# Reordering the first loads of a one-core decoder trunk

## The reference

```
xn = rmsnorm(h, mixer_norm[0])
h  = h + retention(xn, ret_w_in, ret_w_out)      # 4 heads, q and k rotated by cos/sin tables
h  = h + hier_moe(rmsnorm(h, ffn_norm[0]), ...)  # 32 experts, 2 per token
k_sh, v_sh = shared_kv(h, kv_norm, w_kv, k_norm)
h  = h + dilated_attention(rmsnorm(h, mixer_norm[1]), k_sh, v_sh, ...)
h  = h + hier_moe(rmsnorm(h, ffn_norm[1]), ...)
```

## Time and profile before

| | |
|---|---|
| median of 3 runs | 1517.93 us (1515.38 to 1518.26) |
| profiled execution | 1517.55 us, span 1515.7 us |
| TensorE busy | 1186.6 us, 78% of the span |
| VectorE, ScalarE | 434.6 us (29%), 340.7 us (22%) |
| DMA | 489.02 MB, mean 323 GB/s |

### The profile page before, as it was taken

The page is one execution under the profiler, slowest core; times in us unless marked ns, Lnnn a source line. Parts: engine busy times, 40 slices in busy tenths (PEclk is TensorE's granted clock), DMA queues, the critical chain, the costliest instruction groups (busy, mean ns, idle before and its releaser), DMA issues.

```text
span 1515.7 us, 16138 instructions
## 1 busy us (share of the span) xinstructions
PE 1186.6 (78%) x6928; PEld 712.2 (47%) x6928; DVE 434.6 (29%) x834; ACT 340.7 (22%) x560; POOL 64.8 (4%) x119
## 2 busy tenths in 40 slices
PE   4999996858667667576999899996857677577575
PEld 4986785413323133132788767776413133133131
DVE  4754535100100101003766534635100101001001
ACT  3334422101001001012655444642101001001010
POOL 2000000000000000000300051030000000000000
PEclk8999997988878898797999989996988789688888
DMA  8552476999999999998545554457999999999996
GB/s 307 180 195 103 193 277 234 420 421 421 421 421 422 421 421 421 422 421 349 146 167 184 203 110 123 172 168 312 373 421 421 421 421 421 422 421 422 421 421 264
DMA packets 90778, 489.02 MB, mean 323 GB/s; under 512 B 6385, under 2 KB 6449, under 8 KB 41041
## 3 DMA queue, kind: packets, MB, share of 16 engines
q1 hardware_dynamic: 86736, 480.55, 78.7%
q0 software_dynamic: 3968, 7.42, 2.8%
HBM read 486.77 MB, written 1.17 MB: 322 GB/s over the span
## 4 chain that ended last, share of the span: by engine, by line
PE 58%; DMA 34%; DVE 4%; issue 1%; SPq 1%; ACT 1%; POOL 0%; ACTq 0%; DVEq 0%
DMA ring<-in_exp_down 20%; DMA ring_more<-in_exp_down 13%; PE bank L1004 8%; PE triple L1043 7%; PE triple L344 7%; PE triple L345 7%; PE triple L346 7%; PE bank L1079 4%; PE triple L1060 4%; PE bank L1060 2%; PE bank L344 2%; PE bank L346 2%; PE bank L345 2%; DMA ring<-in_ret_w_in 1%; PE bank L1426 1%
## 5 line engine op out<-in xcount | busy, mean ns | idle before, releaser
L1043 PE MATMUL triple<-ring,work 128*32 128x512 f32 x1344 | 251.4, 725 | 84.9 <-DMA ring<-in_exp_up 53.5
L1043 PE MATMUL triple<-ring_more,work 128*32 128x512 f32 x704 | 161.0, 720 | 38.8 <-DMA ring<-in_exp_up 25.6
L1043 PEld LDWEIGHTS triple<-ring,work 128*32 128x32 f32 x1344 | 63.9, 129 | 218.4 <-issue 218.4
L1153 DVE TENSOR_TENSOR work<-work,triple 128x512 f32<-128x512 f32 x16 | 11.0, 688 | 529.3 <-PE triple L1043 529.3
L1060 PE MATMUL triple<-ring,work 128*32 128x512 f32 x344 | 93.8, 910 | 78.5 <-DMA ring<-in_exp_down 41.6
L1004 PE MATMUL bank<-work,hn 128*128 128x128 f32 x512 | 125.8, 407 | 16.5 <-DVE h L1162 12.2
L1004 PEld LDWEIGHTS bank<-work,hn 128*128 128x128 f32 x512 | 123.2, 335 | 27.9 <-issue 23.4
L1162 DVE TENSOR_TENSOR h<-h,bank 128x512 f32<-128x512 f32 x64 | 44.0, 687 | 279.7 <-PE bank L1079 279.7
L326 DVE TENSOR_TENSOR lo_b<-ring,hi_b 128x2048 fp32r<-128x2048 f32 x40 | 90.0, 2288 | 21.3 <-ACT hi_b L319 21.3
L1043 PEld LDWEIGHTS triple<-ring_more,work 128*32 128x32 f32 x704 | 39.2, 128 | 102.9 <-issue 102.9
L1060 PE MATMUL triple<-ring_more,work 128*32 128x512 f32 x168 | 60.2, 922 | 33.4 <-DMA ring<-in_exp_down 29.5
(11 more groups left out here) (280 smaller groups left out, 1791.3 us busy)
## 6 DMA issues: line engine op xcount, KB each, us to landing
ring<-in_exp_down SPq DMA_DIRECT2D x43, 2048.0 KB, 32.6
ring<-in_exp_gate SPq DMA_DIRECT2D x42, 2048.0 KB, 32.9
ring<-in_exp_up SPq DMA_DIRECT2D x42, 2048.0 KB, 33.0
ring_more<-in_exp_gate SPq DMA_DIRECT2D x22, 2048.0 KB, 32.9
ring_more<-in_exp_up SPq DMA_DIRECT2D x22, 2048.0 KB, 33.5
ring_more<-in_exp_down SPq DMA_DIRECT2D x21, 2048.0 KB, 32.5
ring<-in_ret_w_in SPq DMA_DIRECT2D x12, 2048.0 KB, 9.3
ring<-in_w_kv SPq DMA_DIRECT2D x12, 2048.0 KB, 8.8
```

What stands on the lines that cost most here:

```text
L1043: last = nc.tensor.matmul(bank[2 + kind][rows, :], m_x[:, k, rows], w[e][:, kk * FF:(kk + 1) * FF], start=(k == 0), stop=(k == KD - 1))
```

## The change

SyncE now issues x, the first weight tile in two halves with a semaphore each, the rotation tables, and then the other tiles. ScalarE's queue issues the identity and the mixer gains on a semaphore of their own. The rest of the small loads are issued by GpSimd after a wait for the first tile. The splitting of tile 0 is laced with the norm and the transposes: low half 0 before them on VectorE, high half 0 before `x_hi` on ScalarE, the other halves behind. TensorE starts on k = 0, 1 when the first batch of `x_lo` is there. ScalarE takes a root right at the start, from a memset tile. In the router, two pairs of semaphores become one pair.

```diff
+        s_ident = sem("identity_and_first_gain_loaded")
+        s_first = sem("first_half_tile_loaded")
+        s_rot = sem("rotation_tables_loaded")
+        s_one = sem("table_operand_set")
...
         def split_act(act, n, parts=(0, 1)):
+            if n == 0:
+                act.wait_ge(s_ring[0] if 1 in parts else s_first, 16)
             if 0 in parts:
-                act.wait_ge(s_ring[slots_in_order[n]], 16 * loads_through(n))
+                if n > 0:
+                    act.wait_ge(s_ring[slots_in_order[n]], 16 * loads_through(n))
...
-            nc.scalar.activation(root_of_no_use[0:1, i:i + 1], h[0:1, 0, 0:1], ACT.Sqrt, scale=0.0)
+            if i > 0:
+                nc.scalar.activation(root_of_no_use[0:1, i:i + 1], h[0:1, 0, 0:1], ACT.Sqrt, scale=0.0)
...
         def retention_pe(pe):
-            xT_ready(pe, 0)
...
                             if hh == 0 and half == 0 and k % 4 == 0:
                                 half_ready(pe, n, k // 4)
+                            if i == 0 and half == 0 and k % 2 == 0:
+                                pe.wait_ge(s_xT_dve, k // 2 + 1)
...
         def retention_act(act):
-            for n in range(-2, 4):
+            for n in range(-1, 4):
...
         def retention_dve(dve, chain):
-            for n in range(-2, 0):
-                split_next(split_dve, dve, n, DENSE_A - 1)
-            dve.wait_ge(r_tab, 16 * 3)
+            split_next(split_dve, dve, -1, DENSE_A - 1)
+            dve.wait_ge(s_rot, 16)
...
             def decayed(hd):
                 dve.wait_ge(r_s_done, hd + 1)
+                dve.wait_ge(r_tab, 16)
...
-            act.wait_ge(s["top_in"], 1)
-            nc.scalar.activation(m_t[:, 1, 0:2], m_t[:, 1, 0:2], ACT.Exp).then_inc(s["top_out"], 1)
+            act.wait_ge(s["exp_in"], 2)
+            nc.scalar.activation(m_t[:, 1, 0:2], m_t[:, 1, 0:2], ACT.Exp).then_inc(s["exp_out"], 1)
...
         @block.sync
             sp.dma_start(h[:, :, :], x[0].rearrange("(t p) d -> p t d", p=P)).then_inc(s_x, 16)
-            sp.dma_start(kept[:, :], constants[:, 0:C_KEPT]).then_inc(s_small, 16)
-            sp.dma_start(gains[:, 0:4:2, :], mixer_norm ...).then_inc(s_small, 16)
-            sp.dma_start(gains[:, 1:4:2, :], ffn_norm ...).then_inc(s_small, 16)
-            sp.dma_start(gains[:, 4, :], kv_norm ...).then_inc(s_small, 16)
-            for i in range(N_WIN):
+            first = ring[:, 0, :].rearrange("p (k c) -> p k c", k=KD)
+            sp.dma_start(first[:, 0:KD // 2, :], win[:, 0:KD // 2, 0:COLS]).then_inc(s_first, 16)
+            sp.dma_start(first[:, KD // 2:KD, :], win[:, KD // 2:KD, 0:COLS]).then_inc(s_ring[0], 16)
+            sp.dma_start(work[:, 16384:16384 + 2 * S], constants[:, C_COS:C_COS + 2 * S]).then_inc(s_rot, 16)
+            for i in range(1, N_WIN):
                 load_tile(sp, FIRST_WIN + i, win[:, :, i * COLS:(i + 1) * COLS], KD)
...
         @block.gpsimd
-            pool.dma_start(r_cos, constants[:, C_COS:C_COS + S]).then_inc(r_tab, 16)
-            pool.dma_start(r_sin, constants[:, C_SIN:C_SIN + S]).then_inc(r_tab, 16)
+            pool.wait_ge(s_ring[0], 16)
+            pool.dma_start(kept[:, P:C_KEPT], constants[:, P:C_KEPT]).then_inc(s_small, 16)
+            pool.dma_start(gains[:, 1:4:2, :], ffn_norm ...).then_inc(s_small, 16)
+            pool.dma_start(gains[:, 4, :], kv_norm ...).then_inc(s_small, 16)
...
         @block.scalar
+            act.dma_start(kept[:, 0:P], constants[:, 0:P]).then_inc(s_ident, 16)
+            act.dma_start(gains[:, 0:4:2, :], mixer_norm ...).then_inc(s_ident, 16)
+            act.wait_ge(s_one, 1)
+            nc.scalar.activation(root_of_no_use[0:1, 0:1], root_of_no_use[0:1, 1:2], ACT.Sqrt)
             norm_act(act, 0)
-            act.wait_ge(s_small, 64)
+            split_act(act, 0, (0,))
+            act.wait_ge(s_ident, 32)
             transpose_act(act, 0, (x_hi, x_lo), 0)
+            split_act(act, 0, (1,))
             retention_act(act)
+            act.wait_ge(s_small, 16 * 3)
...
         @block.vector
+            nc.vector.memset(root_of_no_use[:, :], 1.0).then_inc(s_one, 1)
             norm_dve(dve, chain, 0)
-            dve.wait_ge(s_small, 64)
+            split_dve(dve, 0, (0,))
+            dve.wait_ge(s_ident, 32)
             transpose_dve(dve, 0, (x_hi, x_lo), 0)
+            split_dve(dve, 0, (1,))
+            dve.wait_ge(s_small, 16 * 3)
             retention_dve(dve, chain)
...
         @block.tensor
-            pe.wait_ge(s_small, 64)
+            pe.wait_ge(s_ident, 32)
             transpose_pe(pe, 0)
```

More of the change, by code:

```diff
@@ L767, in build @@
         for layer in range(2):
-            names = ("logits", "exp_in", "exp_out", "top_in", "top_out", "chosen", "ranked", "slots_ready",
+            names = ("logits", "exp_in", "exp_out", "chosen", "ranked", "slots_ready",
                      "route_w", "step")
@@ L921, in route_dve @@
             V.tensor_tensor(A, hot1, hot2, ALU.add).then_inc(s["chosen"], 1)
-            V.tensor_tensor(m_t[:, 1, 0:2], top2, top1, ALU.subtract).then_inc(s["top_in"], 1)
+            V.tensor_tensor(m_t[:, 1, 0:2], top2, top1, ALU.subtract).then_inc(s["exp_in"], 1)
             psum, r = tmp(TT), tmp(TT)
@@ L926, in route_dve @@
             chain(V.tensor_reduce(psum, m_t[:, 0, 0:8].rearrange("p (t g) -> p t g", t=TT), AX, ALU.add))
-            dve.wait_ge(s["top_out"], 1)
+            dve.wait_ge(s["exp_out"], 2)
             chain(V.tensor_scalar(r, m_t[:, 1, 0:2], 1.0, None, ALU.add))
@@ L1835, in _ @@
             sp.dma_start(h[:, :, :], x[0].rearrange("(t p) d -> p t d", p=P)).then_inc(s_x, 16)
-            sp.dma_start(kept[:, :], constants[:, 0:C_KEPT]).then_inc(s_small, 16)
-            sp.dma_start(gains[:, 0:4:2, :], mixer_norm.rearrange("l (p k) -> p l k", k=KD)).then_inc(s_small, 16)
-            sp.dma_start(gains[:, 1:4:2, :], ffn_norm.rearrange("l (p k) -> p l k", k=KD)).then_inc(s_small, 16)
-            sp.dma_start(gains[:, 4, :], kv_norm.rearrange("(p k) -> p k", k=KD)).then_inc(s_small, 16)
-            for i in range(N_WIN):
+            first = ring[:, 0, :].rearrange("p (k c) -> p k c", k=KD)
[3 more added lines that the diff above has]
+            for i in range(1, N_WIN):
                 load_tile(sp, FIRST_WIN + i, win[:, :, i * COLS:(i + 1) * COLS], KD)
@@ L1879, in route_loads @@
                                ).then_inc(s, 16)
-            pool.dma_start(r_cos, constants[:, C_COS:C_COS + S]).then_inc(r_tab, 16)
-            pool.dma_start(r_sin, constants[:, C_SIN:C_SIN + S]).then_inc(r_tab, 16)
+            pool.wait_ge(s_ring[0], 16)
+            pool.dma_start(kept[:, P:C_KEPT], constants[:, P:C_KEPT]).then_inc(s_small, 16)
+            pool.dma_start(gains[:, 1:4:2, :], ffn_norm.rearrange("l (p k) -> p l k", k=KD)).then_inc(s_small, 16)
+            pool.dma_start(gains[:, 4, :], kv_norm.rearrange("(p k) -> p k", k=KD)).then_inc(s_small, 16)
             pool.dma_start(work[:, 16896:16896 + RET_H * DECAY_W],
@@ L1918, in _ @@
         def _(act):
+            act.dma_start(kept[:, 0:P], constants[:, 0:P]).then_inc(s_ident, 16)
+            act.dma_start(gains[:, 0:4:2, :], mixer_norm.rearrange("l (p k) -> p l k", k=KD)).then_inc(s_ident, 16)
+            act.wait_ge(s_one, 1)
+            nc.scalar.activation(root_of_no_use[0:1, 0:1], root_of_no_use[0:1, 1:2], ACT.Sqrt)
             norm_act(act, 0)
-            act.wait_ge(s_small, 64)
+            split_act(act, 0, (0,))
+            act.wait_ge(s_ident, 32)
             transpose_act(act, 0, (x_hi, x_lo), 0)
+            split_act(act, 0, (1,))
             retention_act(act)
+            act.wait_ge(s_small, 16 * 3)
             norm_act(act, 1)
```

## The result

| | before | changed |
|---|---|---|
| median of 6 runs | 1516.32 us (1514.56 to 1518.26) | 1508.59 us (1506.24 to 1509.72) |
| ratio, 95% interval | | 0.9947 (0.9934 to 0.9960) |
| profiled execution, span | 1517.55, 1515.7 | 1509.11, 1507.3 |

The change makes the kernel 7.7 us faster by the medians, 8.4 by the two spans.

The account below looks back on a forecast made before the run. The start was taken as bound by the order of bytes, with time won before 38 us passing through whole. Earlier resumption 5.76, twelve early matmuls 1.43 and clock 0.5 sum to 7.7: 1510.2 us, range 1506.5 to 1514.0.

Parts of the forecast that it names:

- x: Load of x at the start: lands at 5.3 us instead of 5.73, with about 0.16 MB less ahead of it.
- First half: First half of the first weight tile: lands 2.7 us after x, at 8.0 us; upper bound 10.7.
- Norm: First norm on ScalarE: early root moves the table load, so root and scaling come 1.1 us earlier; hn ready at 8.6.
- Identity and gains: Loads the transposes wait for: mixer gains land at 7.9 us, hidden; at worst 10.5, with 1.4 us reaching TensorE.
- Strand and resumption: VectorE's low part, x_lo, second low part in a row: TensorE resumes at 18.05 us instead of starting at 23.81, gaining 5.76.
- Twelve matmuls: Tile 0 on TensorE: 12 of 96 matmuls done before the stream resumes, worth 1.43 us.
- Clock: TensorE's low clock after the stream resumes: 4.95 us instead of 6.10, worth 0.5 us.
- Rival B: TensorE's clock already up at resumption, tile 1's second half then possibly late: gain 8.1 to 9.95, time 1508.9; chance 0.20.
- What is late next: Tile 1: at worst lands as before, 24.86 us, likely 1 to 2 sooner; its low halves hidden by 0.4.
- Small loads: GpSimd's loads awaited by VectorE before tile 1's low halves: issued by 12.2, landing 19.3 to 21.5 us; cost 0.
- Rival E: Slower through VectorE's wait for small loads: each us of landing beyond 28.0 costs one; up to 1522.2 us; chance 0.05.
- Rival D: No change: a later wait, likely the expert stage's loads, eats the win; gain under 3, time 1516.5; chance 0.06.

Follow-up runs that it names:

- e6: Changed kernel with identity and mixer gains issued on SyncE's queue behind the first tile; 1513.59 us (one execution), kernel before beside it 1516.74.
- e3: Changed kernel with the first weight tile as one 2 MB load instead of two halves; 1512.25 us, kernel before beside it 1516.74.
- e1: Changed kernel without GpSimd's wait for the first tile, so its small loads go at once; 1514.67 us, kernel before beside it 1516.44.
- e7: Changed kernel with ScalarE's early root and its table load back between squares and root; 1514.16 us (one execution), kernel before beside it 1517.04.
- e2: Changed kernel's loads with the old order of work: tile 0's copies and low halves behind the transposes; 1511.83 us, kernel before beside it 1516.74.
- e8: Changed kernel with GpSimd's small loads waiting for the third weight tile instead of the first; 1512.79 us (one execution), kernel before beside it 1517.04.
- e4: Changed kernel with GpSimd's small loads waiting for the fourth weight tile instead of the first; 1517.80 us, kernel before beside it 1516.44.
- e5: Changed kernel with SyncE waiting for x before issuing the first tile; 1510.60 us (one execution), kernel before beside it 1516.74.
- v8: Changed kernel with tile 0's high-weight matmuls first, low-weight last, and x_lo made before both low halves; 1505.38 and 1504.42 us in two runs.

## Why the prediction was right, step by step

The forecast was 7.7 us (1510.2, 1506.5 to 1514.0); the medians gave 7.7 and 6.3. The mechanism holds: order of bytes, the serial strand, the shift handed on one for one. Two terms were mis-sized, against each other: the resumption came 0.6 us late, and the clock gave 1.4 us where I had 0.5. That the sum came out to the tenth is luck. By my own sign, a first copy past 9, the forecast stood on its edge: the copy came at 9.05 and 8.98.

*x.* Forecast to land at 5.3, landed at 6.2. The step failed in two ways. I took 0.16 of the 0.23 MB moved beside x in the first 5.73 us for time that x would win; e6 has neither GpSimd's loads nor the small packets beside x, and x is there at 5.68, no earlier than before. GpSimd's loads never stood ahead of x: in the kernel before their first packet moves at 5.58. And the identity and gains cost it about 0.5 us (e6), where I counted their bytes only.

*First half.* Forecast 2.7 behind x, measured 2.8 (6.25 to 9.05); so at 9.0 instead of 8.0. The halves are worth 2.7 (e3), and the small loads out of the way 4.6 at the first half, 5.1 at the end (e1).

*Norm.* The forecast 1.1 us for the table load is what the root won (2.57 to 1.47). Of it 0.7 reaches the resumption (e7), not all, since the tile's strand is nearly as long.

*Identity and gains.* Taken to land at 7.9; landed at 1.18 (the second issue) + 5.2 = 6.4, hidden.

*Strand and resumption.* Forecast 18.05, came 18.66: 1.0 late from x, 0.4 made up by shorter steps (x_lo 3.22, no pauses).

*Twelve matmuls.* 1.43 forecast; e2 lost 1.4.

*Clock.* I took the middle of two rows, 4.95 us. It was 2.9 in both traces of the changed kernel, outside my two rows, and over the ten traces from the changed kernel to e8 it was 0, 0, 0, 2.9, 2.9, 3.1, 3.7, 4.9, 5.5, 6.1. The term is right in kind (0.45 us per us). Its size is not set by TensorE's work alone, as changed and e4 show; whether it changes between executions of one kernel is not shown, since the only pair of this start agreed. The 6.1 of the kernel before is one trace. With the measured values the sum is (23.81 - 18.66) + 1.43 + (6.1 - 2.9) x 0.45 = 8.0; the trace has 38.06 - 30.12 = 7.9.

*Rival B*, the clock up at the resumption, is real: e4, e5 and e8 show it. Its second half, that tile 1 would then come late, is not: in e4, e5 and e8 the tile landed in time. *What is late next* failed: I let tile 1 land at 22.9 to 24.86, it landed at 18.6. I had let GpSimd's loads run beside it from 12.4; they are issued from 12.05 on, one each 0.5 to 0.7 us, but the first of their packets moves at 16.15 in the trace, so most of tile 1 passed alone.

*Small loads.* Forecast 19.3 to 21.5, landed at 13.43 + 5.1 = 18.5, before VectorE was free (18.60). The Trainium skill's trap "DVE blocks DMA" (SBUF — State Buffer) speaks of certain VectorE instructions; had those of this stretch been of that kind, the prediction's sum would have put the loads at 27. GpSimd issued them in 0.6 to 0.7 us each, and they landed, while VectorE worked all through 12 to 18 us, so this trace does not show the block for these kinds of instruction. *Rival E's* slope was right, its foot of 28.0 a little late: 26.8 with the clock up (e4, e8); with it low as in the changed kernel 30.12 - 2.3 = 27.8, an estimate that no run tests.

*Handing on.* The rest of the span is 1285.9 to 1289.1 us in all traces, 1287.9 before: the shift passes whole, give or take 2 us. Rival D has nothing for it.

## What to carry to other kernels

At the head of a kernel, write down bytes in the order in which they are needed and let everything else wait for a semaphore of the last needed one: here 1.8 MB of loads, nearly all needed only tens of us later, stood for 4.6 us of the start. Then look for the serial strand behind the first bytes and order the arithmetic by what its operands cost: passes that need only the quickly made operand go first (v8, 5.1 us more at tile 1). And read the pace of matmuls from their distance before counting on a clock; behind the gap of 1.6 to 3.4 us the low clock cost 1.3 to 2.8 us in some of these traces and nothing in others.

## What was not expected of the hardware

The printed clock was 1.00 over stretches in which the matmuls ran at half pace (the start of every trace, up to 21.6 us in the changed kernel). The clock fell behind a stretch whose only gap was of 1.04 us (v8, at 62 us). Between the early matmuls and the stream, where the clock had risen before, it fell in the gaps of e7 (3.1 us) and e6 (3.4), while those of e4 and e8 (2.8) and e5 (1.6) left it up. 72 KB in 416 small packets on another queue held a 1 MB load back by about 0.5 us, where their bytes alone are 0.2 us at 388 GB/s. And GpSimd's loads move late: in the five traces that I read for it (before, changed, e1, e4, e8) their first packet comes 3.6 to 4.4 us after the first issue.
